# The prompt's output projection from seven products of quarter blocks instead of eight

## The reference, cut to what matters

```python
D_MODEL = 2048; SEQ = 1024; DEC_SEQ = 64; PAST_LEN = 128; N_HEADS = 8; HEAD_DIM = 128
...
    h = _rmsnorm(x, g)
    proj = h @ w_in
    y_ssm, hT_re, hT_im = _s5_scan(u, ...)
    zs = jax.nn.gelu(y_ssm, approximate=False)
    y_ssm = zs * jax.nn.sigmoid(zs @ w_glu + b_glu)
    y_ssm = _rmsnorm(y_ssm * jax.nn.silu(z_ssm), ssm_ng)
    ...
    o = _fox_block(...)                                   # per head and block of 128 queries
    y_att = _rmsnorm(o * jax.nn.silu(z_att), att_ng)
    y = jnp.concatenate([y_ssm, y_att], axis=-1)          # (tokens, 2048)
    x = x + y @ w_out                                     # w_out is (2048, 2048)
```

## Time and profile before

| | |
|---|---|
| median of 3 runs | 1971.2 us (1968.9 to 1971.32) |
| the profiled execution | 1968.27 us |
| its span, first to last instruction | 1966.6 us |
| granted TensorE clock, mean | 0.998 |
| PE busy | 1935.5 us, 98% |
| DVE busy | 982.3 us, 50% |
| ACT busy | 648.6 us, 33% |
| POOL busy | 408.2 us, 21% |
| DMA | 180.13 MB, mean 92 GB/s |

### The profile page before, as it was taken

One profiled execution on the slowest core, in us unless ns is written; L12 is line 12 of the kernel. 1 busy time (PEld: TensorE's weight loads), 2 busy tenths in 40 slices (PEclk: granted clock), 3 DMA queues, 4 the chain that ended last, 5 costly groups with the idle time before them and its releaser, 6 DMA issues.

```text
span 1966.6 us, 32482 instructions
## 1 busy us (share of the span) xinstructions
PE 1935.5 (98%) x11552; PEld 1808.6 (92%) x11552; DVE 982.3 (50%) x1907; ACT 648.6 (33%) x1265; POOL 408.2 (21%) x707
## 2 busy tenths in 40 slices
PE   5999999999999999999999999999999999999999
PEld 4899999999999999999999999999999988888887
DVE  7865566555453553635546354463575652222221
ACT  6432333333333343334333343334354441111110
POOL 5875455555110010010100101001010021010100
PEclk9999999999999999999999999999999999999999
DMA  8344444344322121131211312112165452222221
GB/s 224 109 119 104 111 111 110 105 115 131 90 60 63 36 70 50 32 87 35 81 35 34 87 32 86 36 36 83 32 230 191 142 195 95 92 93 90 96 89 49
DMA packets 194162, 180.13 MB, mean 92 GB/s; under 512 B 32186, under 2 KB 165396, under 8 KB 192884
## 3 DMA queue, kind: packets, MB, share of 16 engines
q1 hardware_dynamic: 176832, 127.97, 23.6%
q0 software_dynamic: 11744, 40.19, 6.1%
q10 hardware_dynamic: 5524, 11.14, 1.6%
HBM read 133.28 MB, written 45.97 MB: 91 GB/s over the span
## 4 chain that ended last, share of the span: by engine, by line
PE 94%; DVE 4%; DMA 1%; issue 0%; ACT 0%; SPq 0%; POOL 0%; POOLq 0%; DVEq 0%; ACTq 0%
PE GB L193 60%; PE TB L2099 4%; PE TB L2100 4%; PE TB L2101 4%; PE TB L1988 3%; PE TB L2009 3%; PE GB L2099 2%; PE GB L2100 2%; PE GB L2101 2%; PE TB L2030 2%; PE TB L1135 1%; PE TB L1145 1%; PE TB L1146 1%; PE TB L2049 1%; DVE XL L671 1%; PE TB L1974 0%
## 5 line engine op out<-in xcount | busy, mean ns | idle before, releaser
L193 PE MATMUL GB<-XH,whi 128*128 128x384 f32 x2448 | 828.8, 339 | 1.2 <-ACT QR L1555 1.0
L193 PE MATMUL GB<-XH,wlo 128*128 128x384 f32 x2448 | 801.7, 327 | 0.0
L193 PE MATMUL GB<-XL,whi 128*128 128x384 f32 x2448 | 799.0, 326 | 0.0
L193 PEld LDWEIGHTS GB<-XH,whi 128*128 128x128 f32 x2448 | 460.3, 188 | 14.3 <-issue 9.1
L193 PEld LDWEIGHTS GB<-XL,whi 128*128 128x128 f32 x2448 | 460.5, 188 | 5.3 <-issue 3.8
L193 PEld LDWEIGHTS GB<-XH,wlo 128*128 128x128 f32 x2448 | 459.7, 188 | 0.0
L181 DVE TENSOR_TENSOR wlo<-wraw,whi 128x256 fp32r<-128x256 f32 x412 | 201.5, 492 | 484.3 <-ACT whi L177 480.2
L177 ACT CAST whi<-wraw 128x256 fp32r<-128x256 f32 x412 | 166.6, 405 | 642.5 <-PE GB L193 632.8
L1419 POOL DMA_DIRECT2D ya_s<-ZR x7 | 4.0, 575 | 729.9 <-DVE ZR L1793 729.9
L1840 DVE RECIPROCAL SQ<-SQ 128x136 f32<-128x136 f32 x128 | 127.6, 997 | 1.1
L1602 ACT ACTIVATE PR<-PR,nmx 128x128 f32<-128x128 f32 (+8 forms) x72 | 53.4, 742 | 183.9 <-DVE nmx L1811 172.0
(11 more groups left out here) (423 smaller groups left out, 2607.6 us busy)
## 6 DMA issues: line engine op xcount, KB each, us to landing
wraw<-in_w_in SPq DMA_DIRECT2D x380, 128.0 KB, 2.2
OLF<-in_w_out SPq DMA_DIRECT2D x48, 256.0 KB, 3.0
XO<-in_x_prompt POOLq DMA_DIRECT2D x32, 256.0 KB, 4.3
out_y_prompt<-XO POOLq DMA_DIRECT2D x24, 256.0 KB, 3.5
xt<-in_x_prompt SPq DMA_DIRECT2D x5, 1024.0 KB, 5.3
NCB<-nc_s POOLq DMA_DIRECT2D x8, 608.0 KB, 4.8
us_s<-UP SPq DMA_DIRECT2D x8, 548.0 KB, 3.1
U<-us_s SPq DMA_DIRECT2D x64, 68.5 KB, 3.2
```

Of the source, the lines that this page charges most:

```text
L193: ins = T.matmul(group(GB if bank is None else bank, b), w[:, s % SPL, kk], x[:, k + kk, c:c + n], start=first and kk == 0 and i == 0, sto ...
```

## The change

The prompt's 1024 tokens and 2048 channels are cut into four quarters of 512 tokens by 1024 channels, and `w_out` into four quarters of 1024 by 1024. Seven products of such quarters, combined, give the four quarters of the output (Winograd's form of Strassen's algorithm). In the code a product is m = 0 to 6 with the operands A12, A11, S2, S3, S1, S4 and A22. A group g = 0 to 13 is half a product (512 output columns): 8 pieces of weights, each with 4 tiles of 128 tokens. So:

- **Weights.** Four of the seven products need sums of quarters of `w_out`. Beside attention, for each of the 8 heads and twice (c = 0, 1), POOL loads four blocks of 128 x 512 into TS (two DMAs of 512 KB), DVE makes four sums of 512 columns in two pairs at the steps of T_MIX, and POOL writes 1 MB to the scratch tensor t_s. The pieces for these products come from t_s.
- **Tokens.** Sums of quarters of y need both branches normalised first. So the scales are put on a diagonal (DVE, `diagonal`, 1024 columns), spread over the partitions by matmuls with a matrix of ones (PE, `spread`, two of 512 columns in plain float32 per branch) and copied from PSUM by ACT; `norm` multiplies quarters by them (32 of 512 columns on DVE), `mix` makes the sums (40), and the operands are split again by ACT (`opnd_hi`, 48) and DVE (`opnd_lo`, 48) into one of two operand buffers while the product before is multiplied. The first product (A12, the attention channels) is not normalised; its scale goes in when it is taken, as before.
- **Takes.** Each group has 4 accumulators of the prompt, taken in the ways of `take`; the pieces U, V and the four output quarters are put together with `join` and `residual_c21` (24 more additions) and 8 copies on ACT (`copy_u`). 
- **Sample tokens** are multiplied directly, as before: groups 0 to 3 carry one such tile (5 accumulators), and groups 10 and 11 two (6 accumulators), the state-space one with 8 pieces of weights of its own each (`alone`: a piece with only two matmuls). The hi and lo tiles are now written side by side by ACT and DVE, and POOL's copies (`sample_tile`) are gone.
- **The ring** of weight pieces has 6 slots instead of 8, and 14 x 8 + 16 = 128 pieces pass through it instead of 64. ACT runs `out_hi` up to 4 pieces ahead in its list, DVE `out_lo` up to 3. POOL's DMA scratch is set to 8192 bytes.
- `split_ya` and `rest_ya` in the GLU stage handle 512 + 64 columns instead of 1088, and `split_ys`, `rest_ys` are gone.

The matmuls of 512 columns in the output projection are 14 x 8 x 4 x 3 = 1344 for the prompt and 4 x 8 x 2 + 2 x 8 x 4 = 128 for the sample: 1472 instead of 1664.

```diff
-ORING = 6
+ORING = 4
+LEAD_HI, LEAD_LO = 4, 3
...
+    t_s = scratch("t_s", [D_MODEL // 2, 4 * D_MODEL // 2])
...
+            NG2 = 14
+            DUAL = (10, 11)
+            PIECES = [(g, i, alone) for g in range(NG2) for i in range(KG) for alone in ((True, False) if g in DUAL else (False,))]
...
+            ACC0 = [0]
+            for g in range(NG2):
+                ACC0.append(ACC0[-1] + (6 if g in DUAL else 5 if g < 4 else 4))
...
+            A12, A11, S2, S3, S1, S4, A22 = range(7)
...
-            SUM_AT = {1: 1, 4: 0}
+            T_MIX = {True: ((4, 6), (14, 15)), False: ((20, 21), (25, 28))}
+            SUM_AT = {1: 1, 2: 0}
+            SPREAD_AT = {3: 1, 5: 0}
...
+                def out_load(n):
+                    if n >= RAW:
+                        sp.wait_ge(f["lo"], stands["lo"] + n - RAW + 1)
+                    if n < ORING:
+                        sp.wait_ge(e["o_mm"], NR * NH)
+                        sp.wait_ge(e["v_out"], 32 * NH)
+                    elif n < RING:
+                        sp.wait_ge(W.mm, W.multiplied(OUT0 - 1))
                     else:
-                        sp.wait_ge(f["acc"], stands["acc"] + NA * q)
-                    n = q // 2 * NW
-                    sp.dma_start(out_slot(c)[2], w_out_v[:, out_k(c), n:n + NW]).then_inc(W.w_in[c % RAW], 16)
+                        out_freed(sp, n - RING)
+                    sp.dma_start(out_slot(n)[2], out_weights(n)).then_inc(W.w_in[n % RAW], 16)
...
+                def mixed_weights(h, c):
+                    if att_head(h) or c:
+                        pool.wait_ge(e["ts_out"], 16 * (2 * h + c))
+                        stand(pool, "pool")
+                    for a in range(2):
+                        pool.dma_start(TS[:, 2 * a:2 * a + 2],
+                                       w_out[0][ds(h * P + a * D_SSM, P), :].rearrange("r (b c n) -> r b c n", b=2, c=2)[:, :, c]
+                                       ).then_inc(e["ts_in"], 16)
+                    pool.wait_ge(e["ts_d"], 2 * h + c + 1)
+                    stand(pool, "pool")
+                    pool.dma_start(t_s[ds(h * P, P), :].rearrange("r (j c n) -> r j c n", j=4, c=2)[:, :, c], TS[:]
+                                   ).then_inc(e["ts_out"], 16)
...
+                pool.wait_ge(o0, 144)
+                residual("c22", 9, BX[0], x0)
...
+                    pool.wait_ge(f["fin"], 9 + t)
+                    pool.dma_start(rows_of(out, "c12", 10, t), BX[0][:, t]).then_inc(o0, 16)
+                sample_out("sr", 10, o0)
+                residual("c21", 12, UU[0], x1)
+                pool.wait_ge(o0, 288)
+                residual("c12", 11, BX[0], x0)
...
+                def copy_u(g, t):
+                    act.wait_ge(f["ev"], stands["ev"] + acc_of(g, t) + 1)
+                    act.wait_ge(f["mix"], stands["mix"] + mix_s3(KG - 1))
+                    S.copy(UU[g % 2][:, t], out_bank(acc_of(g, t))).then_inc(f["u_copy"], 1)
...
+                for n, (g, i, alone) in enumerate(PIECES):
+                    if n < 5:
+                        continue
+                    while done <= min(n + LEAD_HI, len(PIECES) - 1):
+                        out_hi(done)
+                        done += 1
+                    if alone:
+                        continue
+                    if g == 1:
+                        sample_ys(i)
+                        opnd_hi(0, i, quarter(0, i, 0), mix_q11(i))
...
+                    if g in (3, 4) and i < 2:
+                        copy_u(g - 1, 2 * i)
+                        copy_u(g - 1, 2 * i + 1)
+                    if 1 <= g <= 4 and i == 1:
+                        take_low(g - 1, sample_of(g - 1), acc_of(g - 2, "a") if g > 1 else None)
+                    if g in (11, 12):
+                        if i == 0:
+                            take_low(g - 1, "s", acc_of(3, "s") if g == 11 else acc_of(10, "a"))
+                        if i == 1:
+                            take_low(g - 1, "a", acc_of(g - 1, "s"))
...
+                def mixed_weights(h, c, n):
+                    if n == 0:
+                        dve.wait_ge(e["ts_in"], 32 * (2 * h + c + 1))
+                        stand(dve, "dve")
+                        o.then(V.tensor_tensor(TS[:, 1], TS[:, 3], TS[:, 1], ALU.subtract))
+                        o.then(V.tensor_tensor(TS[:, 0], TS[:, 1], TS[:, 0], ALU.add))
+                    else:
+                        V.tensor_tensor(TS[:, 2], TS[:, 0], TS[:, 2], ALU.subtract)
+                        V.tensor_tensor(TS[:, 3], TS[:, 3], TS[:, 0], ALU.subtract).then_inc(e["ts_d"], 1)
...
+                def norm(w, k, half):
+                    dve.wait_ge(f["r_copy"], stands["r_copy"] + 2 - w)
+                    if k == KG - 1:
...
+                    n = slice(HALF * half, HALF * (half + 1))
+                    V.scalar_tensor_tensor(quarter(w, k, half), y_raw(w, k)[:, n], y_gain(w, k), RR[w][:, n], ALU.mult, ALU.mult
+                                           ).then_inc(f["mix"], 1)
...
+                    V.tensor_tensor(dst, a, b, op).then_inc(f["mix"], 1)
...
+                    V.tensor_tensor(opnd(XLR, which, k, 1), src, opnd(XLR, which, k, 0).bitcast(f32), ALU.subtract).then_inc(f["alo"], 1)
...
+                    dve.wait_ge(f["tmp"], stands["tmp"] + nth + 1)
+                    o.then(V.scalar_tensor_tensor(x, TMP, scale, x, ALU.mult, ALU.add))
+                    V.scalar_tensor_tensor(x, out_bank(acc_of(g, t), slice(0, DEC)), scale, x, ALU.mult, ALU.add).then_inc(f["ev"], 1)
...
+                    if m == 4:
+                        dve.wait_ge(f["x_in0"], 160 + 64 * c)
+                        V.tensor_tensor(BX[0][:, t], acc, BX[0][:, t], ALU.add).then_inc(f["mid"], 1)
+                        V.tensor_tensor(UU[c][:, t], acc, UU[c][:, t], ALU.add).then_inc(f["ev"], 1)
+                    if m == 5:
+                        dve.wait_ge(f["x_in0"], 288 + 64 * c)
+                        V.tensor_tensor(BX[0][:, t], acc, BX[0][:, t], ALU.add).then_inc(f["ev"], 1)
...
+                def join(g, t):
+                    if g // 2 == 4:
+                        dve.wait_ge(f["mid"], 4 * (g % 2) + t + 1)
+                        V.tensor_tensor(BX[0][:, t], BX[0][:, t], VV[g % 2][:, t], ALU.add).then_inc(f["fin"], 1)
...
+                done = 8
+                for n, (g, i, alone) in enumerate(PIECES):
+                    if n < 5:
+                        continue
+                    while done <= min(n + LEAD_LO, len(PIECES) - 1):
+                        out_lo(done)
+                        done += 1
+                    if alone:
+                        continue
+                    if g >= 1 and i < 2:
+                        if i == 0 and g - 1 in DUAL:
+                            take_sample(g - 1, "s", 4 + 2 * (g - 11))
+                        take(g - 1, 2 * i)
+                        take(g - 1, 2 * i + 1)
+                    if i == 2:
+                        if 1 <= g <= 4:
+                            take_sample(g - 1, sample_of(g - 1), g - 1)
+                        if g - 1 in DUAL:
+                            take_sample(g - 1, "a", 5 + 2 * (g - 11))
+                        if 9 <= g <= 12:
+                            for t in range(4):
+                                join(g - 1, t)
+                    if g == 0:
+                        for k in ((0, 1, 2), (3, 4, 5), (6, 7))[i - 5]:
+                            norm(1, k, 0)
+                            norm(1, k, 1)
+                    if g == 1:
+                        norm(0, i, 0)
+                        if i:
+                            opnd_lo(A11, 0, i - 1, quarter(0, i - 1, 0))
+                        sample_lo(0, i)
...
+                    if g == 5:
+                        if i == 0:
+                            opnd_lo(S3, 0, KG - 1, quarter(0, KG - 1, 0))
+                        mix(quarter(0, i, 1), quarter(0, i, 1), quarter(1, i, 1), ALU.add, mix_s2(KG - 1))
+                        mix(quarter(1, i, 0), quarter(1, i, 0), quarter(1, i, 1), ALU.subtract, mix_s2(KG - 1))
...
+                    if g in (11, 13) and i in (4, 5):
+                        for t in (2 * i - 8, 2 * i - 7):
+                            residual_c21(g // 13, t)
...
+                    for b in range(2):
+                        ins = T.matmul(TB[:, 1024 + NW * b:1024 + NW * (b + 1)], onesr[:].bitcast(f32),
+                                       DD[w][:, 4 * b:4 * b + 4].rearrange("p m c -> p (m c)"), start=True, stop=True)
+                    ins.then_inc(f["r_mm"], 1)
...
+                for n, (g, i, alone) in enumerate(PIECES):
+                    slot = out_slot(n)
+                    pe.wait_ge(f["lo"], stands["lo"] + n + 1)
+                    if alone:
+                        sample_block(g, i, "s", slot)
+                        continue
+                    if g % 2 == 0:
+                        pe.wait_ge(f["alo"], stands["alo"] + opnd_at(g // 2, i))
```

(13 more changed lines are left out.)

555 lines of the change are left out of this document (352 added, 203 removed).

## The result

The changed kernel takes 1949.57 us (median of 4 runs, 1945.97 to 1951.70), the kernel before 1970.05 in the same comparison: ratio 0.9895, 95% interval 0.9883 to 0.9908, 20.5 us faster. I had forecast 1945, with 1931 to 1962 around it. The profiled run took 1948.71, with a span of 1947.1 against 1966.6.

The account below looks back on a forecast made before the run. PE was taken to bound the output projection: 357.4 us instead of 384.7 (matmuls, sums, spread, waits, slow clock), -27.3. With attention +2.0 and GLU -1.0, -26.3 against the median 1971.2 gave 1944.9, forecast as 1945, range 1931 to 1962.

Parts of the forecast that it names:

- PE bounds the stage matmul by matmul: Output projection: each matmul less saves 0.2274 us while other engines keep up; 192 fewer give -43.7 us.
- DVE as the bound (2040): Rival, output projection: DVE's 360 instructions at 1.26 us each make the stage 454 us; chance 0.06, shared with other losses.
- a wait and a slow stretch at every change of group (1968): Rival, output projection: nine more group boundaries at 1.0 and 1.6 us cost 23 us; chance 0.11.
- Waits at groups 1, 10, 11 and 12: Output projection, changes of group: PE waits 2.5, 1.0, 6.7 and 1.5 us, 11.7 in all.
- The second part of group 11: Output projection, group 11: two lo parts and a rest stand ahead of the next take, 1.8 us more wait.
- The residual loads must be back before a take: Output projection, after `join`: stores and loads take some 12 us, next need at least 16 us away; no cost.
- One more slow stretch: Output projection: a wait like group 11's may drop PE's clock, 1.6 us allowed.
- The rival beside it: Output projection: each change of group costs a wait and a slow stretch, 23 us, giving 1968; chance 0.11.
- Attention +2.0: Weight sums on DVE beside attention cost 0.3 us for each of 7 heads, 2.0 in all; bounds 0 and 19.
- the shortfall of 0.45 at steps 14 and 15: Attention: both pairs of sums, 2.7 us, precede the copy to PT with slack 2.25; part falls into idle time.
- GLU -1.0: GLU stage: ACT splits 512 + 64 columns instead of 1088, so PE's 1.03 us wait should go, -1.0 us.
- The signs of being wrong: PE idle at most group changes, L1926 waits within groups, clock drops elsewhere, heads over 0.5 us longer, DVE instructions above 0.8.

Follow-up runs that it names:

- the repeat: The changed kernel run again without any edit, compared with the kernel before: 1948.51 us, ratio 0.9892.

## Why the prediction was right, and where it was not

1. **PE bounds the stage matmul by matmul, 0.2274 each.** Right. The table leaves 0.3 us over in 342.5, and 96 fewer matmuls took 21.6 us out of groups 4 to 9, where the count says 21.8. The rivals with DVE as the bound (2040) and with a wait and a slow stretch at every change of group (1968) are out: DVE's instructions of 512 columns take 0.67 to 0.74 each, and groups 2 to 9 have no wait at all in any of the profiles with all matmuls.
2. **Waits at groups 1, 10, 11 and 12.** Right in place, releaser and size: 2.4 idle for 2.5, 5.1 for 4.9, 1.5 for 1.5. They came from walking the lists with durations of before. That the list's order was the cause is shown by moving it: the wait of group 1 vanished, and group 11's wait for the sample's take (L2129) shrank to 2.2 with the copy moved a piece earlier and to 0.5 with the copy ahead of the cast that waits for a load. There 2.5 for the prompt's takes (L2158) came in its place, until these were moved too. The second part of group 11, forecast at 1.8, was at most 0.2: 7.0 less 5.1 idle and 1.7 slow clock. That PE at the lower clock gave DVE the time for it is likely, and not shown.
3. **"The residual loads must be back before a take ... the next need is at least 16 us away."** This step failed, as a wait put at nothing. The way from `join` to the loads' landing was priced at some 12 us and measured 13.5 (1874.2 to 1887.7), in part by luck: this residual goes to another buffer than the one that is stored from, and does not wait for the stores to land (3.5 in the sum), and the last load took 8.0 instead of 4.3. The need was looked for among the takes. The lower left residual is needed at pieces 4 and 5 of the same group, 6 us after `join` begins. It cost 5.6 us, where the stage came out 5.2 above the forecast. With the sums a group later 3.1 of the idle 4.9 were gone; the other 1.8 are the pieces' own loads, which I had taken as in time after the first piece.
4. **One more slow stretch.** There were two more, the second behind the wait of step 3. The Trainium skill's "TensorE: Matmul & The Clock Gate" ("HAM oscillation — how this bites in real kernels") says that a wait for data can put PE back to half clock, again at each such wait. The traces agree for the long waits: every one of 3.3 us and more had a slow stretch behind it, the shorter ones only at times (see below). The rival beside it failed in its count, since groups 2 to 9 had no waits that could bring one.
5. **Attention +2.0.** Too much: it was 0.6 to 0.7, and the experiment without the sums gives it all back. How much of the shortfall of 0.45 at steps 14 and 15 fell into idle time was an estimate, and too careful.
6. **GLU -1.0.** Only 0.3 came, since most of the wait stays: PE still waits 0.80 for ACT's QR (before 1.03). My reason, the columns that ACT has to split, is at most a small part of it; what sets the wait was not tried.

```profile
1520.22 0.41 PE L195 MATMUL GB<-XH,whi 128*128 128x384 f32 x1 [0.80 <-ACT QR L1723]
```

7. **The start.** 2.4 us of the profiled run are chance of the first 80 us, in code that neither kernel changes: the same early matmul starts at 63.21 in it, and at 60.32 both in the repeat and before.
8. **The signs of being wrong.** Two of those named came once each: a wait for a lo part (L1926) within a group, and a clock below 1 behind it. Both are step 3.

So the profiled run was to be 1942.0 and was 1948.7: +5.2 from the stage, +2.4 from the start, +0.7 from the GLU, -1.4 from attention, and -0.2 behind the last matmul and outside the span. The median, 1949.6, is 4.6 above the forecast, about the size of step 3. That the errors in attention and GLU partly cancel is luck.

Of 43.7 us of matmuls the changed kernel keeps 20.5. With the matmuls of one column spread in both kernels and the changed one's lists put in order (1967.35 and 1931.83, on one chip) it keeps 35.5: 43.7 less 3.4 for `spread`, 3.4 of waits and 0.7 in attention would be 36.2.

## What to carry to other kernels

When an engine that bounds a stage loses work, walk the in-order lists of its suppliers at each change of phase, with durations from the trace of before: it gave four waits out of five to within half a microsecond. For every load ask who reads it first, and look among all readers, not among those of the kind at hand; a consumer that waits for a DMA blocks everything queued behind it. Place what frees a buffer ahead of any instruction that itself waits for a load.

## What the runs showed of the hardware

- Matmuls of one column bring the granted clock down from 2.4 to 1.2 GHz though PE is busy: 20 of them in two batches (each of these plain float32 matmuls shows as two records) were followed by one or two stretches of 1.6 to 1.8 us loss in eight profiles of nine, and by none in the four profiles where they stand two to four behind each tile, in both kernels. In two of the four this was the only edit.
- Idle PE and the clock: waits of 3.3 us and more (fifteen in eight profiles, up to 6.1) were each followed by a stretch at the lower level. The same wait of 2.4 in group 1 had one behind it in two profiles of seven. Both of 2.2 had one; those of 2.6 and of 1.9 and less had none, and 2.5 had one in one kernel and none in the next. So two runs of one kernel can differ by whole stretches of 1.7 to 3 us. Most of the spread of 1946 to 1952 can be that; it is not shown, since only one run in each comparison has a profile.
- Beside the pieces' loads, with the DMA engines 98% busy from 1880 to 1890 us, the last of four loads of 256 KB took 8.0 us from its start (1879.70) to its landing (1887.7), where the profile page's median for such a load is 4.9.
